# Two blocks of layers with an expert gather, one core: the second block sent through in two passes of 256 tokens

## The reference, cut to what matters

```python
h = rms_norm(x, norm1_w) * (1.0 + scale1) + shift1
aq, ak, av, gq, gk, gv, gg, glr = split(h @ w_in)               # 2320 columns
att = sliding_window_attention(aq, ak, av, sinks)               # window of 128, 8 heads on 2 key heads
log_a = log_sigmoid(glr @ gate_up + gate_bias) / 16
go = gla_chunked(gq, gk, gv, log_a)                             # linear attention, decays over all earlier tokens
go = rms_norm(go, gla_norm_w) * silu(gg)
x = x + gate1 * (concat(att, go) @ w_out)
h2 = rms_norm(x, norm2_w) * (1.0 + scale2) + shift2
q = h2 @ wq                                                     # 8 heads, 2 x 128
...                                                             # 16 best of 128 x 2 sub-keys, 16 best sums: 128 experts per token
hid = gelu(einsum('tkd,td->tk', u[expert], h2)) * gates
x = x + gate2 * einsum('tk,tkd->td', hid, v[expert])
return rms_norm(x, final_norm_w)
```

## Time and profile before

| | |
|---|---|
| median of 3 runs | 2601.83 us (2595.57 to 2604.07) |
| span of the profiled execution | 2733.2 us, 131.4 us over that median |
| bytes moved | 665.46 MB, 536.94 of them by the indirect DMAs |
| DMA engines' share of the span in those | 52.1% |
| busy: PE, DVE, POOL, ACT | 2263.1, 1475.1, 1188.2, 645.8 us |

### The profile page before, as it was taken

How to read it: one execution, slowest core, us unless ns; L and a number is a source line. 1 busy time by engine, 2 the same in 40 slices (tenths; PEclk the granted TensorE clock), 3 DMA queues, 4 the chain that set the end, 5 groups by cost and what they waited for, 6 DMA issues and landing times.

```text
span 2733.2 us, 27506 instructions
## 1 busy us (share of the span) xinstructions
PE 2263.1 (83%) x9564; PEld 1445.1 (53%) x9564; DVE 1475.1 (54%) x3398; ACT 645.8 (24%) x1548; POOL 1188.2 (43%) x1128
## 2 busy tenths in 40 slices
PE   7999999999999999896977776767777777676775
PEld 6876888889979877665532222322223222232222
DVE  2435232375573425779866664557654567644434
ACT  3225332421120435422121111111111211111111
POOL 5200222110000221325566666666676666766664
PEclk9999999999999999898989998999988999988899
DMA  4211131144452222048889999999999999999998
GB/s 140 78 47 63 63 123 70 70 175 173 186 201 91 78 78 78 32 175 311 310 333 354 359 363 363 367 367 355 363 374 354 358 379 364 373 364 367 372 362 308
DMA packets 170936, 665.46 MB, mean 243 GB/s; under 512 B 19632, under 2 KB 20160, under 8 KB 160320
## 3 DMA queue, kind: packets, MB, share of 16 engines
q0 software_dynamic: 147456, 536.94, 52.1%
q1 hardware_dynamic: 23360, 127.00, 12.7%
HBM read 661.76 MB, written 2.10 MB: 243 GB/s over the span
## 4 chain that ended last, share of the span: by engine, by line
PE 42%; POOL 20%; DVE 15%; issue 10%; another core or an unknown queue 9%; ACT 2%; DMA 1%; SPq 0%; POOLq 0%; DVEq 0%; ACTq 0%
POOL area L544 11%; PE bank L1034 9%; PE bank L1035 9%; PE bank L1036 9%; POOL weights L535 8%; DVE weights L1925 6%; PE bank L1489 4%; PE bank L1076 2%; PE bank L1132 2%; PE bank L1187 1%; PE bank L1206 1%; PE bank L1093 1%; PE bank L1115 1%; PE bank L1099 1%
## 5 line engine op out<-in xcount | busy, mean ns | idle before, releaser
L1431 PE MATMUL bank<-area,gain_row 128*128 128x512 f32 x1888 | 967.3, 656 | 368.5 <-issue 204.2
L1431 PEld LDWEIGHTS bank<-area,gain_row 128*128 128x128 f32 x1888 | 366.6, 207 | 962.3 <-issue 824.1
L1925 DVE CUSTOM_DVE_ANT_0 weights<-weights,bank 128x1024 f32<-128x1024 f32 x504 | 596.9, 1218 | 346.7 <-DMA weights<-in_peer_u,scratch 241.0
L544 POOL DMA_INDIRECT area<-in_peer_v,scratch x512 | 491.5, 960 | 269.4 <-issue 142.3
L535 POOL DMA_INDIRECT weights<-in_peer_u,scratch x504 | 482.5, 957 | 261.4 <-issue 146.7
L918 ACT ACTIVATE gain_row<-ident,scratch 128x128 f32<-128x128 f32 x472 | 178.5, 398 | 1082.8 <-remote 588.7
L463 POOL CAST weights_split<-weights 128x2048 fp32r<-128x2048 f32 x25 | 47.7, 1906 | 851.1 <-DMA weights<-in_w_in 508.1
L1034 PE MATMUL bank<-h_T_high,weights_split 128*128 128x512 f32 (+1 forms) x544 | 211.6, 389 | 0.4 <-POOL weights_split L464 0.4
L1035 PE MATMUL bank<-h_T_low,weights_split 128*128 128x512 f32 (+1 forms) x544 | 209.7, 386 | 0.0
L1036 PE MATMUL bank<-h_T_high,weights_split 128*128 128x512 f32 (+1 forms) x544 | 209.7, 385 | 0.0
L1545 DVE CAST weights_split<-weights 128x2048 fp32r<-128x2048 f32 x41 | 50.4, 1228 | 209.0 <-DMA weights<-in_w_ff 122.8
(11 more groups left out here) (310 smaller groups left out, 3010.3 us busy)
## 6 DMA issues: line engine op xcount, KB each, us to landing
weights<-in_w_ff SPq DMA_DIRECT2D x32, 1024.0 KB, 4.8
scratch<-in_w_ada SPq DMA_DIRECT2D x48, 512.0 KB, 6.5
weights<-in_w_in SPq DMA_DIRECT2D x22, 1024.0 KB, 4.8
area<-in_w_pq SPq DMA_DIRECT2D x4, 2048.0 KB, 9.4
area<-in_peer_v,scratch POOLq DMA_INDIRECT x512
weights<-in_peer_u,scratch POOLq DMA_INDIRECT x504
weights<-in_w_mk SPq DMA_DIRECT2D x4, 1024.0 KB, 4.8
weights<-in_w_out SPq DMA_DIRECT2D x4, 1024.0 KB, 4.8
```

The lines of the kernel that those rows point to most:

```text
L544: pool.indirect_dma_start(vring[k], None, A["peer_v"], index).then_inc(v_landed[k], 16)
L1431: ins = pe.matmul(bank[half][:], wdiag[:, (done + i) % 4, :], vring[r % RING][:, half * COLS:(half + 1) * COLS], start=(first and i == 0), ...
L1925: dve.tensor_tensor_reduce(out=up_slot(b, r), in0=up_slot(b, r), in1=token[b][:], scale=1.0, scalar=0.0, op0=ALU.mult, op1=ALU.add, accum_ ...
```

## The change

The first block keeps its order on every engine. The second block is written anew, as a generator `work(p)` for each engine, which is run for pass p = 0 (token blocks 0 and 1) and p = 1 (blocks 2 and 3). Pass 0 runs alone; from its end on, pass 1 is laid along the row stream: `along(work(1), rows())` runs a piece of pass 1 and then rows up to the row number that `mark` gives for the end of that piece (about row 15 after the norm, 72 after `w_in`, 93 after window attention, 121 after linear attention, 182 at the end).

- Every weight chunk of the second block (10 of `w_in`, 4 of `w_out`, 8 of the queries) is loaded once per pass, in halves of 0.5 MB, into 4 slots of a half. All are split: the high part by ACT, the low part by POOL for one half in each of the first 18 chunks and by DVE for all others. All products are `three`, 256 columns wide.
- Window attention is 16 units per pass. Linear attention has 9 levels per pass, the last of which, in pass 0, only scales the keys for pass 1 (`kfar`); its product with the queries, which nothing reads, is left out. Pass 1 adds four groups of products of its queries with the keys of pass 0.
- The token rows lie in SBUF, not in PSUM. They are rebuilt from high and low parts.
- The rings have 6 slots for u rows and 5 for v rows. `LAG` is 56. PE's loops are gone: the rows are written out.
- `between` has new places; the last two steps of `pick` for block 0, quarter 1, come ahead of the first dot.

```diff
-RING = 8
-LAG = 88
+RU, RV = 6, 5
+LAG = 56
...
+ORDER = []
+for _p in range(2):
+    ORDER += [(_p, "in2", i) for i in range(len(IN2))] + [(_p, "out2", i) for i in range(4)] + [(_p, "wq", i) for i in range(8)]
+POOL_LOW = [2 * c for c in range(FIRST[1] - 4)]
...
+        def along(work, rows):
+            n = 0
+            for want in work:
+                while n < want:
+                    next(rows)
+                    n += 1
+            for _ in rows:
+                pass
...
+            for n in range(ROWS + LAG):
+                if n >= LAG:
+                    down_row(n - LAG)
+                if n < ROWS:
+                    up_row(n)
...
-                dve.tensor_tensor_reduce(out=up_slot(b, r), in0=up_slot(b, r), in1=token[b][:], scale=1.0, scalar=0.0,
+                dve.tensor_tensor_reduce(out=uring[k], in0=uring[k], in1=token[:, b % 2, :], scale=1.0, scalar=0.0,
                                          op0=ALU.mult, op1=ALU.add, accum_out=hid[:, r:r + 1]).then_inc(u_free[k], 1)
...
+                if l < 8:
+                    dve.tensor_tensor(to[0], q, f, ALU.mult)
+                    ins = dve.tensor_tensor(to[1], k, f, ALU.mult)
+                elif p == 0:
+                    ins = dve.tensor_tensor(kfar[:], k, f, ALU.mult)
...
+            def rows():
+                for step in (2, 3):
+                    pick(0, 1, step)
+                for n in range(ROWS):
+                    between(n // SLOTS, n % SLOTS)
+                    hidden(n)
+                    yield
+            for _ in work(0):
+                pass
+            along(work(1), rows())
```

## The result

The changed kernel takes 2765.47 us (median of 4 runs, 2745.70 to 2775.18), against 2602.62 (4 runs, 2595.57 to 2604.07) for the kernel before, timed beside it: a ratio of 1.0637, 95% interval 1.0585 to 1.0689. It is slower by 163 us. Predicted were 2755 and a range of 2650 to 2870.

What follows compares the result with a forecast made beforehand. It took DMA bytes to bound the row stream from the first v row, and DVE the stretch before. Terms 57 + 60 + 25 + 20 = 162 us on the span, 154 on the median, gave 2755 us, range 2650 to 2870.

Steps and rivals of the forecast that it cites:

- steps 1 and 2: Up to the v rows: first gather at 1166 us, 35 earlier; first v row at 1320, 39 earlier, DVE setting that stretch.
- step 3: Row stream after the first v row: 32 more gathers at 1.449 us and 49 us of reloaded weights make the span 57 longer.
- step 4: Beside u rows 56 to 182: pass 1 brings PE to 425 us against 414 of bytes and weights; 60 us taken.
- signs of being wrong: Wrong if: first gather before 1110, share 0.95 all through pass 1, issues still 0.94, or ring waits costing more than pass 1.
- step 5: POOL's issues beside dots with the token in SBUF: 0.21 us longer each, 216 if all shows; 25 us taken.
- step 6: Rings cut from 16 to 11 slots: POOL runs less far ahead and waits more, 0 to 162 us; 20 taken.
- The scaling by 0.952: Span to median: 2601.83 / 2733.2 = 0.952, by which the 162 us on the span became 154 on the median.
- second rival: Gathers: POOL becomes the bound by the port rule, 1.615 us each against 1.449; 298 us more, 2886; chance 0.13.
- only bytes count: Rival for the row stream: only the 57 us of remaining bytes show, pass 1 slips in beside the rows; 2656; chance 0.20.

Runs made afterwards that it cites:

- the pair on slower chips: Unedited changed kernel on a slower chip, 2840.55 us (span 2835.7), set against the unedited kernel before, timed again, 2746.96 us (span 2734.3).
- the repeat: The kernel before, timed and profiled again with no edit on a slower chip: 2746.96 us beside 2744.91, ratio 1.0006.

## Why the prediction was right, and where not

The time was right (2755 against 2765), in part by luck, as will be seen: two parts of the sum missed by some 60 us each, in opposite directions. The sign was right for the reason given: the earlier start doesn't pay for what the stream gets. Step by step:

- **First gather and first v row** (steps 1 and 2): 1166 predicted and 1166.0 measured, 1320 and 1310.4. (The step's own numbers, 50 of 56 rows in 130 us from 1193 on, make 1309 and not 1320.) The claim that DVE sets the stretch between holds (115.29 of 119.40 us busy).
- **The remaining bytes** (step 3, +57): of its three parts, 46 for 32 gathers less a head start of 39 is near (47 less 46 in the pair on slower chips). The 49 for weights is wrong. The step read a DMA share of 0.96 at 363 GB/s as full engines. With 22 MB more the engines did up to 411, at no cost. On slower chips this term was 0 by the added loads and 16 by the loads left out.
- **Pass 1 on PE** (step 4, +60): the size is near, the reason wrong. Beside pass 1 the rows lose 74 us against before in the pair on slower chips, and that is the step's place and length. But PE's sum of over 100% was not it: with a third of the products left, nothing changed. One of the prediction's own signs of being wrong showed as well: the DMA share beside pass 1 was 0.96, where it wanted less than 0.9 (PE was busy 0.89 of it). POOL's account of the stretch has the time: issues with a mean of 1.18 us where they took 0.96, 56 us on 248, and 58 us of waits for slots, less what before waited in as many gathers. The 56 are step 5's mechanism and not step 4's. For the waits I have an argument and no proof: the weave keeps PE and DVE away from a sum or a dot for some us at a time, and a ring of 5 or 6 slots doesn't cover that. Only the ring was tried, not the order of the weave, and a shorter ring lengthened the waits after pass 1 as well.
- **Gathers beside dots** (step 5, +25): right in kind, too small. Putting half of the tokens back into PSUM gave 46 us back on a faster chip; putting three quarters of them into SBUF cost 32 on a slower one. The step's own 0.21 us per issue was nearly right (0.16 measured in the mean: 180 us on all issues, from 19 before, where the step had 216). I had let 216 us of it hide behind the bytes' pace, and that pace was wrong for the chips that the result was timed on: there, by the estimate below, it was 1.31 and not 1.45. The rule cited from the Trainium skill ("SBUF — State Buffer", "SBUF: two separate sides"), that the later of the two fully blocks, agrees with the trace: an issue of 1.76 us ends 0.80 after the DVE operation that it met. It fits less well the other way round: an issue that came first did not keep DVE off for its 0.93 us.
- **Shorter rings** (step 6, +20): two slots fewer cost 26, so 20 for five is hardly too much. The step from 16 to 11 itself wasn't tried.
- **The scaling by 0.952** was a step too, and it was wrong: 2733.2 was a span on a slower chip. On a slower chip, whose rows the steps use, their sum of +162 stands against 101 measured. On a faster one, where the result was timed, it stands against 163, and the factor took 8 of it away for no reason.

With the faster chips' times this can be closed as an estimate. If before has its first v row at 1357 and its tail of 17 there too, 2602.6 leaves 1227 us for 936 gathers, 1.311 each (a guess, since no trace of the kernel before was taken on a faster chip). The changed kernel has 255 to 1740 us at 1.685 (+95), then 713 at 1.404 (+66), 42 for the 32 moved and 47 of head start: +156, of 158 by this profile's span (and 163 by the medians). So steps 4 to 6, 105 together, measure 161 there, and step 3, 57, measures about -5: two errors of some 60 us that cancel. The total was hit with luck, and the 0.952, which has no ground, hardly moved it. Of the 161, two fifths lie after pass 1, where POOL's own pace is the bound. That is the second rival's mechanism. It had a chance of 0.13 and a pace of 1.615, while 1.404 was measured, so its price was too high, but for the part after pass 1 it names the cause. That 46 us of it go away with half of the tokens in PSUM is shown; the rest of the 161 is put down to its causes by POOL's account alone.

Of "only bytes count", the other large rival, nothing is left: it would have given 2656.

**What stays open.** Why the gathers go at 1.45 us on slower chips with room in the engines. The profiles there show waits with an unseen releaser (before: POOL L544 101.6 us in the repeat), and those of the changed kernel on faster chips show none (on a slower one 30.8), but what they wait for isn't shown. Whether weights would cost bytes on a faster chip, where the engines reach 408 GB/s once POOL lets them. And what writing PE's rows out is worth: no run has the changed kernel with loops.

None of the changed kernel's versions beats the kernel before. Of those on the faster chip the best, with half the tokens in PSUM, is 4.8% slower (1.0482, 1.0440 to 1.0524); it was not timed on a slower one, where the changed kernel itself is 3.8% slower.

## What to carry to other kernels

A full DMA share is no proof that bytes are the bound (22 MB more beside a share of 0.95 cost nothing on the slower chips): add some, and see whether the time moves, before weights or moved rows are priced by the byte. Where gathers are issued by POOL at nearly the stream's pace (here 0.94 and a gap of 0.30 against 1.31, an estimate, or 1.45), the home of the other operand of a DVE operation beside them is a term of its own: moving it from PSUM to SBUF cost 0.12 to 0.16 us per gather. And before a span is set against a median, make sure that both are from one chip; only ratios to a kernel timed beside it carry over.

## What the runs showed of the hardware, unexpected

- Two kinds of chips: the kernel before took 2591 to 2603 us or 2733 to 2745, the changed one 2765 to 2769 or 2841. The changed kernel's first gather goes out at 1166.0 on one and at 1163.1 on the other, so it is the time after it, the row stream, that differs.
- Direct loads on SyncE's queue went through beside indirect gathers at no cost, 411 GB/s together, while the gathers alone got 363. The Trainium skill ("SBUF — State Buffer", "SBUF: two separate sides") puts the DMA side's peak at about 436 GB/s; 411 is the most that a slice showed here.
- POOL's issue is held up if it starts inside a DVE operation with two SBUF operands, and then until that one's end and 0.80 us more (392 of the 395 issues over 1.00 us in the changed kernel's profile). Such operations are not the only ones: an issue of 1.24 us at 1607.89 started inside a DVE multiplication of one SBUF tensor of 1024 columns by a column (L1665) and ended 0.80 after it. One that starts ahead of it takes its 0.93 us undisturbed, so two engines that trigger each other can fall into a step where nearly nothing is lost (0.07 us in 2.5).
